# Dilated attention one half of heads at a time, with alternating banks

## The reference

```python
DIL_PAIRS = ((128, 1), (512, 4), (2048, 16))      # two heads each
def one_block(args):
    idx = q_pos[:, None, None] - offsets[None, :, None] * dil[None, None, :]
    valid = idx >= 0
    ...
    z = jnp.einsum('bqhd,bqmhd->bqhm', q_blk, k_g).astype(jnp.float32) * scale
    z = jnp.where(valid.transpose(0, 2, 1)[None], z, -jnp.inf)
    z_max = jnp.max(z, axis=-1, keepdims=True)
    p = jnp.exp(z - z_max)
    denom = jnp.sum(p, axis=-1)
    o = jnp.einsum('bqhm,bqmhd->bqhd', p.astype(v.dtype), v_g) / denom[..., None]
    return o.astype(q.dtype), z_max[..., 0] + jnp.log(denom)
...
alpha = jax.nn.softmax(lse, axis=2)               # over the three dilations
return (o * alpha[..., None]).reshape(bsz, seq, n_heads * dh)
```

## Time and profile before

| | |
|---|---|
| median of 3 runs | 1806.86 us (1806.7 to 1807.46) |
| profiled execution | 1804.83 us |
| its span | 1802.7 us |
| TensorE busy | 1742.9 us (97%) |
| VectorE busy | 1138.4 us (63%) |
| ScalarE busy | 693.8 us (38%) |
| GpSimd busy | 396.2 us (22%) |
| dilated attention, first mask matmul to first matmul of "OUT2" | 1334.07 to 1375.57 us of the span |

### The profile page before, as it was taken

The page is one execution under the profiler, slowest core; times in us unless marked ns, Lnnn a source line. Parts: engine busy times, 40 slices in busy tenths (PEclk is TensorE's granted clock), DMA queues, the critical chain, the costliest instruction groups (busy, mean ns, idle before and its releaser), DMA issues.

```text
span 1802.7 us, 22183 instructions
## 1 busy us (share of the span) xinstructions
PE 1742.9 (97%) x7834; PEld 1404.8 (78%) x7834; DVE 1138.4 (63%) x1474; ACT 693.8 (38%) x967; POOL 396.2 (22%) x170
## 2 busy tenths in 40 slices
PE   7999999999999899999999999999988899999997
PEld 6888788888887765878888888787547788888886
DVE  5566777776666765577777666473755577777222
ACT  4123444443224235344444322332563444444221
POOL 3444100001444330310000144444101300000343
PEclk9999999999999999999999999899999899999999
DMA  4232222224663220133222465222100132322331
GB/s 182 98 112 93 93 98 100 93 93 154 231 210 99 76 71 1 59 105 104 94 93 96 156 225 210 95 94 86 44 1 25 69 105 93 101 97 93 105 105 70
DMA packets 52042, 186.25 MB, mean 103 GB/s; under 512 B 5776, under 2 KB 5904, under 8 KB 51984
## 3 DMA queue, kind: packets, MB, share of 16 engines
q1 hardware_dynamic: 50832, 182.47, 29.9%
q10 hardware_dynamic: 1152, 2.99, 0.5%
HBM read 183.35 MB, written 2.10 MB: 103 GB/s over the span
## 4 chain that ended last, share of the span: by engine, by line
PE 88%; DVE 8%; ACT 2%; issue 2%; DMA 1%; ACTq 0%; DVEq 0%; POOL 0%; SPq 0%
PE ps L1479 26%; PE ps L1481 26%; PE ps L1480 26%; DVE RAB L1079 1%; PE ps L1692 1%; PE ps L1758 1%; PE ps L1791 1%; PE ps L1614 1%; PE ps L1615 1%; PE ps L1616 1%; DMA X<-x_in 1%; PE ps L1699 1%; DVE stat L1185 1%; DVE acc L891 1%; PE ps L1718 0%
## 5 line engine op out<-in xcount | busy, mean ns | idle before, releaser
L507 POOL TENSOR_TENSOR WL<-raw,WH 128x1024 fp32r<-128x1024 f32 x157 | 385.1, 2453 | 1358.8 <-ACT WH L556 1358.8
L1479 PE MATMUL ps<-XH,WH 128*128 128x512 f32 x1496 | 587.4, 393 | 15.4 <-DVE XL L902 10.1
L1480 PE MATMUL ps<-XL,WH 128*128 128x512 f32 x1496 | 583.5, 390 | 0.0
L1481 PE MATMUL ps<-XH,WL 128*128 128x512 f32 x1496 | 583.4, 390 | 0.0
L556 ACT ACTIVATE WH<-raw 128x1024 fp32r<-128x1024 f32 x291 | 308.3, 1060 | 581.3 <-PE ps L1481 545.9
L1479 PEld LDWEIGHTS ps<-XH,WH 128*128 128x128 f32 x1496 | 281.8, 188 | 78.7 <-POOL WL L507 9.9
L1481 PEld LDWEIGHTS ps<-XH,WL 128*128 128x128 f32 x1496 | 281.7, 188 | 59.1
L1480 PEld LDWEIGHTS ps<-XL,WH 128*128 128x128 f32 x1496 | 281.8, 188 | 58.6 <-issue 1.0
L1481 PE MATMUL ps<-HH,WL 128*128 128x512 f32 x528 | 205.4, 389 | 0.0
L1480 PE MATMUL ps<-HL,WH 128*128 128x512 f32 x528 | 205.4, 389 | 0.0
L1479 PE MATMUL ps<-HH,WH 128*128 128x512 f32 x528 | 205.4, 389 | 0.0
(11 more groups left out here) (264 smaller groups left out, 1967.8 us busy)
## 6 DMA issues: line engine op xcount, KB each, us to landing
raw<-w_tiles SPq DMA_DIRECT2D x291, 512.0 KB, 3.2
ada<-ada_tiles SPq DMA_DIRECT2D x32, 512.0 KB, 5.1
trig<-ada_tiles SPq DMA_DIRECT2D x16, 512.0 KB, 6.7
out_x<-X SPq DMA_DIRECT2D x8, 256.0 KB, 2.0
X<-x_in ACTq DMA_DIRECT2D x2, 512.0 KB, 8.4
X<-x_in SPq DMA_DIRECT2D x2, 512.0 KB, 8.7
RAB<-c_in SPq DMA_DIRECT2D x2, 512.0 KB, 4.4
MK<-mask_in ACTq DMA_DIRECT2D x1, 576.0 KB, 5.0
```

Source lines behind the costliest of these rows:

```text
L507: nc.gpsimd.tensor_tensor(WL[k % SPL][:, :], raw[:, k, :], f32(WH[k % SPL][:, :]), ALU.subtract).then_inc(s_lo, 1)
L1479: mm(bank, h, xh, start=first, stop=False)
L1480: mm(bank, h, xl, start=False, stop=False)
L1481: return mm(bank, lo, xh, start=False, stop=last)
```

## The change

TensorE computes the logits of one unit in a call, where one call did both units of a class. Unit u + 2 is begun as soon as the exponential of unit u has read the bank, where class r + 1 waited for both exponentials of class r. `window_logits(0)` and `window_logits(1)` stand together where `window_logits(0)` of both halves stood. ScalarE does exponential and normalisation in turn for each unit, where it did two of the one and two of the other. VectorE does one maximum ahead of each copy, where it did two ahead of a copy; and the sum of unit 0 comes ahead of the maximum of unit 1. `window_values` and the high and low parts are as before, in the same places. No buffer, bank or transfer changes.

```diff
@@ -852,17 +852,15 @@
                         act.wait_ge(s_aux, AUX_YA + c + 1)
                         nc.scalar.activation(XH[:, c, :], ps[2 + c][:, :], ACT.Copy).then_inc(s_y2h, 1)
             window_exp(0)
+            window_norm(0)
             window_exp(1)
-            window_norm(0)
             window_norm(1)
             pair_hi(B_HEADS // 2 - 1)
-            for r in range(1, 4):
-                for u in (2 * r, 2 * r + 1):
-                    window_exp(u)
-                for u in (2 * r, 2 * r + 1):
-                    window_norm(u)
-                if r >= 2:
-                    class_hi(r - 2)
+            for u in range(2, 8):
+                window_exp(u)
+                window_norm(u)
+                if u in (5, 7):
+                    class_hi((u - 5) // 2)
             class_hi(2)
             class_hi(3)
             residual("OUT2", 1, None, N_F2)
@@ -1422,22 +1420,18 @@
                             .then_inc(s_y2l, 1)
                 if b == BLOCKS_B + 2:
                     window_max(0)
+            window_sum(0)
             window_max(1)
-            window_sum(0)
             window_sum(1)
             pair_lo(B_HEADS // 2 - 1)
-            for r in range(4):
-                if r < 3:
-                    window_max(2 * r + 2)
-                    window_max(2 * r + 3)
-                window_copy(2 * r)
-                if r < 3:
-                    window_sum(2 * r + 2)
-                window_copy(2 * r + 1)
-                if r < 3:
-                    window_sum(2 * r + 3)
-                if r >= 2:
-                    class_lo(r - 2)
+            for u in range(8):
+                if u < 6:
+                    window_max(u + 2)
+                window_copy(u)
+                if u < 6:
+                    window_sum(u + 2)
+                if u in (5, 7):
+                    class_lo((u - 5) // 2)
             class_lo(2)
             class_lo(3)
             residual("OUT2", 1, None, None, N_F2, gate=2, then=T0["UP2"] + 1)
@@ -1792,24 +1786,19 @@
                    WT[c % 3][:, 0:S - kb * P], start=kb == 3, stop=True, skip_group_check=True)\
                     .then_inc(s_bo, 1)
 
-            def window_logits(r):
-
-                for first in BANKS_Z:
-                    mm(ps[first], mask16[:, 0, :], MK[:, r * S:(r + 1) * S], start=True, stop=False,
-                       skip_group_check=True)
-                    mm(ps[first + 1][:, 0:2 * P], mask16[:, 0, :], MK[:, 4 * S:4 * S + 2 * P], start=True, stop=False,
-                       skip_group_check=True)
-                for i, first in enumerate(BANKS_Z):
-                    half = i * HD
-                    mm(ps[first], FT[half:half + HD, 0, r::4], FT[half:half + HD, 3, :], start=False, stop=True,
-                       skip_group_check=True)
+            def window_logits(u):
+
+                r, half, first = u // 2, u % 2 * HD, BANKS_Z[u % 2]
+                mm(ps[first], mask16[:, 0, :], MK[:, r * S:(r + 1) * S], start=True, stop=False,
+                   skip_group_check=True)
+                mm(ps[first + 1][:, 0:2 * P], mask16[:, 0, :], MK[:, 4 * S:4 * S + 2 * P], start=True, stop=False,
+                   skip_group_check=True)
+                mm(ps[first], FT[half:half + HD, 0, r::4], FT[half:half + HD, 3, :], start=False, stop=True,
+                   skip_group_check=True)
                 for g in (1, 2):
-                    for i, first in enumerate(BANKS_Z):
-                        half = i * HD
-                        last = mm(ps[first + 1][:, (g - 1) * P:g * P], FT[half:half + HD, g, r::4],
-                                  FT[half:half + HD, 3 + g, r::4], start=False, stop=True, skip_group_check=True)
-                        if g == 2:
-                            last.then_inc(s_cz, 1)
+                    last = mm(ps[first + 1][:, (g - 1) * P:g * P], FT[half:half + HD, g, r::4],
+                              FT[half:half + HD, 3 + g, r::4], start=False, stop=True, skip_group_check=True)
+                last.then_inc(s_cz, 1)
 
             def block_of(n):
                 return slice(n * P, (n + 1) * P)
@@ -1847,6 +1836,7 @@
                     pe.wait_ge(s_zb, BLOCKS_B)
                     pe.wait_ge(s_y2l, 4)
                     window_logits(0)
+                    window_logits(1)
                 stick(b)
 
 
@@ -1877,14 +1867,13 @@
                         if g == 2:
                             last.then_inc(s_co, 1)
 
-            for r in range(4):
-                if r < 3:
-                    pe.wait_ge(s_cp, 2 * r + 2)
-                    window_logits(r + 1)
-                window_turn(2 * r)
-                if r > 0:
-                    window_values(r - 1)
-                window_turn(2 * r + 1)
+            for u in range(8):
+                if u < 6:
+                    pe.wait_ge(s_cp, u + 1)
+                    window_logits(u + 2)
+                window_turn(u)
+                if u % 2 == 0 and u > 0:
+                    window_values(u // 2 - 1)
             window_values(3)
 
             out_product("OUT2", (XH, XL), lambda k: pe.wait_ge(s_y2l, 5 if k < 5 else 9))
```

## The result

| | median | runs | lowest to highest |
|---|---|---|---|
| before | 1805.14 us | 20 | 1801.79 to 1807.62 |
| after | 1808.56 us | 20 | 1804.81 to 1816.1 |

The change makes the kernel slower: by 3.4 us in the medians, which is 0.19%. The ratio on record is larger, 1.0029 with a 95% interval of 1.0018 to 1.0039. The three runs shown at first had a median of 1806.86; seventeen more put the kernel before at 1805.14. The profiled execution of the changed kernel took 1806.05 us, with a span of 1803.9 (before 1804.83 and 1802.7).

A forecast was written before the change was run, and what follows sets the result against it. TensorE, busy 97% of the first part's span, was taken as the bound: +8.8 us logits work, -3.0 half-clock time, -4.3 idle time filled give +1.5 on 1806.86, so 1808.4; range 1805.2 to 1811.2.

The forecast's parts named there:

- Within 0.2%: Whole kernel: a change under 3.6 us, about what a measurement can't tell from none; chance 0.79.
- Cost of a half's logits: TensorE, dilated-attention stage: a half alone takes 2.52 us against 2.85 for a pair, 8.8 us more work.
- C: Rival, half's logits: weight loads exposed, 2.95 us a half, total 1811.0, slower; chance 0.06.
- D: Rival, half's logits: weight loads cheap when alone, 2.1 us a half, total 1805.9; chance 0.13.
- E: Rival, half's logits: a half costs half the pair, 1.43 us, total 1802.1, faster by 4.7; chance 0.07.
- the four steps: TensorE's 128-column logits products: strided weight load sets the step, paired or not; eight products take 1.08 us in four steps.
- the second half's product for 0.13: 512-column logits products: pairing adds the second half for 0.13 us, four instructions taking 1.25 against 1.12 for two unpaired.
- The order of events: Start times through the stage: turn 1 at 1352.36, TensorE never waiting until turn 5 at 1368.09, output product at 1377.08.
- The price at full clock: Dilated-attention stage without the clock term: +8.8 us logits work, -4.3 from TensorE idle time that fills.
- -3.0 because no half-clock stretch is left in my chain: Stage: class 2's logits, values 2 and turn 7, slowed by half clock before, run at full clock; saves 3.0 us.
- one of the signs of being wrong: Profile after: the forecast is wrong if the clock falls inside the stage; no 0.50 expected between 1345 and 1377.
- Rival B: Stage's tail gaps: clock falls again, 1.5 us a stretch; once 1809.9, chance 0.14; twice 1811.4, slower, chance 0.08.

The follow-up runs named there:

- packed: Changed kernel with a class's queries from 128 adjacent columns instead of every fourth (other queries' logits): 1808.28 us against 1804.92, ratio 1.0026.
- again_c: The changed kernel as it is, third further look for the profile of a long run: 1808.67 us.
- again_b: The changed kernel as it is, second further look for the profile of a long run: 1809.81 us.
- split: Changed kernel with the orders of before on ScalarE and VectorE, so only TensorE's queue is changed: 1821.43 us against 1805.15, ratio 1.0097.
- nap_halves: Changed kernel with TensorE made to wait for GpSimd sums ahead of the first logits: 1818.67 us against 1804.96, ratio 1.0070.
- nap_pairs: Kernel before with TensorE made to wait for GpSimd sums ahead of the first logits: 1809.72 us, ratio 1.0028.
- orders: Kernel before with only ScalarE's and VectorE's orders changed, logits still in pairs: 1806.77 us against 1805.15, ratio 1.0009.

## Why the prediction was right, and where it was not

The predicted time, 1808.4, stands beside a median of 1808.56; the range held it. The size of the change was less well met. +1.5 was forecast, and the medians differ by 3.4. "Within 0.2%" was given 0.79: the medians, at 0.19%, are just inside it, while the ratio on record, +0.29% (0.18 to 0.39), is most likely outside. That the time agrees within 0.2 us is luck: the base that it was put on, 1806.86, was 1.7 above the later median of 1805.14, and on that median the forecast would have been 1806.6.

*Cost of a half's logits: right.* 2.53 for 2.52, from the rows on the paired and the unpaired product. Rivals C (2.95), D (2.1) and E (1.43) fall by this one number. The reason that I gave for the four steps, the strided load, was wrong (packed): the steps are the same with loads of 196 ns. So was "the second half's product for 0.13": a half's own 512-column product takes 1.24 and the pair's 1.25, and the 0.12 to the unpaired 1.12 of the earlier trace rows goes away in packed, where the stride is gone. The value held since it was taken from the pair's own steps.

*The order of events: right.* Copy 0 was worked out for 1351.27 and stands at 1351.25; turn 1 1352.36 and 1352.35; TensorE busy throughout to turn 5, at 1368.09 and 1368.37; output product 1377.08 and 1377.49, of which 0.15 is a later start of the stage. The new wait of max 1 behind sum 0 is there. In the profiled executions the stage grew by 1.77 for 1.5.

*The price at full clock: right.* 8.8 us of TensorE work less 4.3 of idle time filled is 4.5; the filled kernels differ by 4.7. (In the profiled executions the stage's idle time falls by 3.8, from 8.40 to 4.60.)

*"-3.0 because no half-clock stretch is left in my chain": the step that failed in size.* For the profiled execution it held: 2.9 lost before, none after. For the runs it did not. The clock fell inside the stage in two of four profiles, one of the signs of being wrong that the prediction named. Filling the waits takes 2.8 off the kernel before and 1.9 off the changed one in the medians (1808.42 to 1806.56), so that over the runs the term is about -1 and not -3. 4.7 - 1 = 3.7 is close to the 3.4 measured. In the means, which carry the long runs, filling takes 2.0 off the one and some 2.5 off the other: there the term is about nothing. Both are differences between kernels timed on different chips, and no interval is at hand for them. Rival B named this cost, and said that a stretch is 1.5; in again_c it was 1.6, in again_b 2.5. With halves the clock stayed down for 6.8 us (again_b), 3.4 (again_c), 6.8, 6.8 and 10.2 (split), 13.7 and 10.2 (nap_halves). With pairs it was 3.4 each time in the kernel before and in nap_pairs, and 6.8 and 3.4 in orders. I took the length of a stretch from the kernel before, and it was too short for the changed one.

*The long runs* (9 of 33, some 7 us over the rest) were in no step of the prediction. Their mean clock is lower by 0.003 to 0.006, which is 5 to 11 us of lost time in 1810, and nap_halves makes long runs at will (1818 to 1819.5 in three of four, of which the nap itself is some 3.4). That they are half-clock time in the stage is therefore likely; no long run's profile was had, so it isn't shown, nor is the place where they begin.

## What to carry to other kernels

Two products on different 64-row parts of the array ran in the time of one; a schedule that takes them apart to start each sooner pays the second one in full, here 8.8 us of TensorE for about 4 of idle time. Before a stage is made finer, price its work at full clock and its half-clock time apart: after the same wait it was 3.4 us in one kernel and 13.7 in the other. And where short waits remain in a stage, a few unread matmuls in free banks may be worth more than a better order: 2.8 us here, for some dozen added lines.

## What the runs showed of the hardware

- After a nap the granted clock came back after 3.42 us in the kernel with pairs and after 13.65 in the one with halves, and there it fell again after 10.24 us in which TensorE was busy 9.20. A trace that shows TensorE busy does not by that show its clock safe.
- The Trainium skill (TensorEngine Tiling (Array Packing), Key Properties) says that different tiles can load weights and run matmuls in parallel. The trace agrees: two instructions of 512 columns in 1.24, four in 1.25.
- Weight loads with a stride of four elements took 318 ns and with none 196 (128 columns of float32, 64 rows); the products of 128 columns behind them were not quicker for it, nor slower at half clock (1.04 for four against 1.01).
